# Key pages turned during the projections, a float32 forget gate, and VectorE in place of GpSimd in the 31-tap convolution

## The reference, cut to what matters

```python
# layer 0
h = rmsnorm(x, norm_mix0) @ w_in0              # gb, gc, hv, q, k, v, fl
y_a = gb * causal_dwconv(gc * hv, hist, conv_a_w)          # 3 taps
q, k = rmsnorm(q, q_norm), rmsnorm(k, k_norm)  # per head, 8 heads of 64
logf = log_sigmoid(fl + b_forget)              # fl: 8 columns of w_in0
y_b = attend(q, k, v, cumsum(logf))            # prompt: causal over 512 rows
                                               # samples: 16 pages of 128 cached keys each, and 4 new rows
x = x + concat(y_a, y_b) @ w_out0
x = x + conv_ffn(x)
# layer 1
a, g = split(rmsnorm(x, norm_mix1) @ w_pw1 + b_pw1)
u = a * sigmoid(g)
y = causal_dwconv(u, hist, conv_c_w)           # 31 taps, depthwise
x = x + silu(layernorm(y + conv_c_b)) @ w_pw2
x = x + conv_ffn(x)
```

## Time and profile before

| quantity | value |
|---|---|
| time, median of 3 runs | 1434.85 us (1431.5 to 1435.65) |
| the profiled execution's own time | 1429.25 us |
| its span | 1427.5 us |
| PE busy | 1380.1 us (97%) |
| DVE busy | 726.2 us (51%) |
| ACT busy | 441.8 us (31%) |
| POOL busy | 636.9 us (45%) |

### The profile page before, as it was taken

The page is one execution under the profiler, slowest core; times in us unless marked ns, Lnnn a source line. Parts: engine busy times, 40 slices in busy tenths (PEclk is TensorE's granted clock), DMA queues, the critical chain, the costliest instruction groups (busy, mean ns, idle before and its releaser), DMA issues. The chain is left out here.

```text
span 1427.5 us, 34112 instructions
## 1 busy us (share of the span) xinstructions
PE 1380.1 (97%) x13885; PEld 1292.8 (91%) x13885; DVE 726.2 (51%) x1236; ACT 441.8 (31%) x675; POOL 636.9 (45%) x402
## 2 busy tenths in 40 slices
PE   6998999999999999999999999988999999999998
PEld 5897777768999999999999987768999999999998
DVE  5654778774455443014443499878654430144411
ACT  4243433332333222322223432236332221222221
POOL 3322464443426554445545554432365544455441
PEclk9999999999999999999999999999999999999999
DMA  6415999988143322333314555540333223333131
GB/s 189 134 55 192 310 340 386 378 275 302 46 120 93 88 81 83 91 100 89 88 56 97 147 150 142 146 119 23 109 104 88 81 78 93 103 90 88 55 95 67
DMA packets 259649, 191.57 MB, mean 134 GB/s; under 512 B 26287, under 2 KB 219264, under 8 KB 259528
## 3 DMA queue, kind: packets, MB, share of 16 engines
q1 hardware_dynamic: 258283, 187.71, 42.9%
q0 software_dynamic: 656, 2.13, 0.5%
q10 hardware_dynamic: 605, 0.24, 0.1%
HBM read 173.03 MB, written 6.04 MB: 125 GB/s over the span
## 5 line engine op out<-in xcount | busy, mean ns | idle before, releaser
L711 POOL TENSOR_TENSOR w_l<-w_raw,w_h 128x1024 fp32r<-128x1024 f32 (+2 forms) x195 | 440.0, 2259 | 374.2 <-ACT w_h L883 356.2
L1892 PE MATMUL banks<-xa_h,w_h 128*128 128x272 f32 x1856 | 388.3, 290 | 0.4 <-issue 0.3
L1892 PE MATMUL banks<-xa_h,w_l 128*128 128x272 f32 x1856 | 384.8, 289 | 0.0
L1892 PE MATMUL banks<-xa_l,w_h 128*128 128x272 f32 x1856 | 383.4, 288 | 0.0
L1892 PEld LDWEIGHTS banks<-xa_h,w_h 128*128 128x128 f32 x1856 | 293.5, 189 | 2.4 <-issue 0.8
L1892 PEld LDWEIGHTS banks<-xa_l,w_h 128*128 128x128 f32 x1856 | 292.5, 189 | 0.0
L1892 PEld LDWEIGHTS banks<-xa_h,w_l 128*128 128x128 f32 x1856 | 290.5, 189 | 0.0
L883 ACT ACTIVATE w_h<-w_raw 128x1024 fp32r<-128x1024 f32 (+2 forms) x193 | 185.3, 961 | 195.5 <-PE banks L1892 185.8
L1892 PE MATMUL banks<-h_h,w_h 128*128 128x272 f32 x928 | 192.6, 289 | 0.5 <-DVE x L1643 0.5
L1892 PE MATMUL banks<-h_h,w_l 128*128 128x272 f32 x928 | 192.7, 289 | 0.0
L1892 PE MATMUL banks<-h_l,w_h 128*128 128x272 f32 x928 | 192.1, 288 | 0.0
(11 more groups left out here) (291 smaller groups left out, 1618.2 us busy)
## 6 DMA issues: line engine op xcount, KB each, us to landing
w_raw<-in_w_up SPq DMA_DIRECT2D x88, 512.0 KB, 3.7
k_grp<-in_cache_k SPq DMA_DIRECT2D x128, 256.0 KB, 4.6
v_pg<-in_cache_v SPq DMA_DIRECT2D x120, 256.0 KB, 5.6
w_raw<-in_w_in SPq DMA_DIRECT2D x24, 512.0 KB, 6.5
w_raw<-in_w_down SPq DMA_DIRECT2D x32, 384.0 KB, 3.3
w_raw<-in_w_pw SPq DMA_DIRECT2D x24, 512.0 KB, 4.1
w_raw<-in_w_down SPq DMA_DIRECT2D x32, 320.0 KB, 3.1
w_raw<-in_w_out SPq DMA_DIRECT2D x8, 512.0 KB, 5.4
```

What stands on the lines that cost most here:

```text
L711: g.tensor_tensor(w_l[:, slot, 0:n], w_raw[:, slot, 0:n], w_h[:, slot, 0:n].bitcast(F32), ALU.subtract).then_inc(s_lo, 1)
L1892: ins = mm(out[:, half, 0:HT], w, v[:, half * HT:(half + 1) * HT], start=first and t == 0 and n == 0, stop=last and t == phase.tiles - 1 a ...
```

## The change

1. `forget_gate` multiplies `x` itself, in full float32, by `fw_g`, the forget columns times the gain of the norm (made once by GpSimd). The 544 rows are cut into four parts of 136 (QT), and part c writes to partitions 32c to 32c+7 of one bank, so there are 32 instructions in place of 48.
2. Group 1 of the keys is loaded when slab 9 is done (two slabs earlier in `s_slab`), and VectorE turns it after slabs 10 and 11. The squares of the last head pair are summed right after those of the last but one, in another pair of banks (`last_sums`). Round 0 begins with the scores; its rows of v follow them, and the wait for the last slab's scaling stands behind the scores.
3. In the 31-tap stage SP makes the copies of `u` ahead of the weight loads; VectorE makes the low parts (two a chunk) and the tap weights (one a chunk), and `combine` is split in two, so that its first half (`taps_summed`) runs before a low part. GpSimd has only one low part and the copies for the first and the last chunk left in the loop.

The diff, cut to its core:

```diff
 LAG = 4
-ROWS_IN = {0: ((0, 1), (2,), (3, 4)), 1: ((5, 6), (7,), (8, 9))}
+ROWS_IN = {0: ((), (0, 1, 2), (3, 4)), 1: ((5, 6), (7,), (8, 9))}
...
                     elif slot == 1:
-                        sp.wait_ge(s_slab, ph["qkv"].slab1)
+                        sp.wait_ge(s_slab, ph["qkv"].slab1 - 2)
...
                 i, j = s // 4 % 4, s % 4
+                if s >= 8 and s % 2 == 0:
+                    shifted(s // 2 - 4)
...
                     n_out.extend((before_rows, n_out[0]))
-                if s >= 8 and s % 2 == 0:
-                    shifted(s // 2 - 4)
...
                 split_low(0, slot, DC)
-            pool.wait_ge(s_fw, 33)
-            g.tensor_tensor(fw_l[:, :, :], fw[:, :, :], fw_h[:, :, :].bitcast(F32), ALU.subtract).then_inc(s_fw, 1)
+            pool.wait_ge(s_fw, 32)
+            pool.wait_ge(s_gnd, 1)
+            g.tensor_tensor(fw_g[:, :, :], fw[:, :, :], params[:, 0:DC].unsqueeze(2).to_broadcast([P, DC, NH]), ALU.mult)\
+             .then_inc(s_fw, 1)
...
-            def tap_weights(c, b):
-
-                if isinstance(c, int) and c == 0:
-                    pool.wait_ge(s_cz, 2)
-                    pool.wait_ge(s_hist, 1)
-                    pool.wait_ge(s_tap, 16)
-                if not (isinstance(c, int) and c < 2):
-                    pool.wait_ge(s_cvp, c - 1)
-                g.tensor_tensor(w_sh[b][:, :, :], every32[:, :].unsqueeze(1).to_broadcast([P, 32, 32]),
-                                tap_sh[:, ds(c, 1), :, :].rearrange("p a q k -> p (a q k)").unsqueeze(2)
-                                .to_broadcast([P, 32, 32]), ALU.mult).then_inc(s_wsh, 1)
-
...
-            def turn(i, last):
-                for j in range(4):
-                    if last and j == 2:
-                        for late in (2, 3):
-                            ahead(split_low, ph["pw1"], i, late, last)
-                        tap_weights(i * 2 + 1, 1)
-                        shifted_also(DC - 1)
-                    if last and j >= 2:
-                        continue
-                    ahead(split_low, ph["pw1"], i, j, last)
-                    if isinstance(i, int) and i == 0:
-                        if j == 1:
-                            shifted_also(0)
-                        if j < 2:
-                            tap_weights(j, j)
-                    elif j % 2:
-                        tap_weights(i * 2 + j // 2, j // 2)
-            turns(pool, ph["pw1"], turn, 1)
+            split_low(ph["pw1"].slab0 // 4, 3, DC)
+            shifted_also(0)
+            shifted_also(DC - 1)
+            pool.wait_ge(s_lo, ph["pw2"].slab0 + 3)
...
                 A(sq[:, m % 2, :], x[:, m, :], ACT.Square).then_inc(s_sq, 1)
-            act.wait_ge(s_fw, 32)
-            A(fw_h[:, :, :], fw[:, :, :], ACT.Copy).then_inc(s_fw, 1)
...
                     q_blocks(0)
-                if n >= 4:
+                if 4 <= n < 11:
                     head_root(n - 4)
+                if n == 10:
+                    head_root(7)
...
                 dve.wait_ge(s_misc, 5)
-                V.tensor_tensor(fz[:, 0:HT], bank[0][0:NH, 0:HT], r_all[0:NH, 0:HT], ALU.mult).then_inc(s_dve, 1)
-                st.tick()
-                V.tensor_tensor(fz[:, HT:T], bank[1][0:NH, 0:HT], r_all[0:NH, HT:T], ALU.mult).then_inc(s_miscd, 1)
+                for c in range(4):
+                    at, rows = slice(c * QT, (c + 1) * QT), slice(32 * c, 32 * c + NH)
+                    V.tensor_tensor(fz[:, at], bank[0][rows, 0:QT], r_all[rows, at], ALU.mult)\
+                     .then_inc(s_miscd if c == 3 else s_dve, 1)
+                    if c < 3:
+                        st.tick()
...
                     forget_in()
-                if n >= 4:
+                if 4 <= n < 11:
...
                     forget_sums()
-                if n >= 4:
+                if n == 10:
+                    head_var(7)
+                if 4 <= n < 11:
                     head_norm(n - 4)
+                if n == 10:
+                    head_norm(7)
+                    key_turned(1, 0)
+                if n == 11:
+                    key_turned(1, 1)
...
                     V.memset(bank[1][:, 160:161], 1.0).then_inc(s_clr, 1)
-                if more:
+                if more and n:
                     key_turned(n + 1, 0)
-                if n == 0:
-                    key_turned(1, 1)
...
+            def low_part(s):
+
+                slot = s % 4
+                dve.wait_ge(s_hi, s + 1)
+                dve.wait_ge(s_lo, s)
+                V.tensor_tensor(w_l[:, slot, :], w_raw[:, slot, :], w_h[:, slot, :].bitcast(F32), ALU.subtract).then_inc(s_lo, 1)
+
+            def tap_weights(c):
+
+                if c == 0:
+                    dve.wait_ge(s_cz, 2)
+                    dve.wait_ge(s_tap, 16)
+                if c >= 2:
+                    dve.wait_ge(s_cvp, c - 1)
+                V.tensor_tensor(w_sh[c % 2][:, :, :], every32[:, :].unsqueeze(1).to_broadcast([P, 32, 32]),
+                                tap_sh[:, c, :, :].rearrange("p q k -> p (q k)").unsqueeze(2).to_broadcast([P, 32, 32]),
+                                ALU.mult).then_inc(s_wsh, 1)
+
...
                 dve.wait_ge(s_u, c * 2 + 2)
+                first = 2 * c + ph["pw1"].slab0 + SLOTS
+                if c:
+                    taps_summed(c - 1, 1 - b)
+                else:
+                    tap_weights(0)
+                    tap_weights(1)
+                low_part(first)
...
                     combine(c - 1, 1 - b)
+                if 1 <= c < DC - 1:
+                    tap_weights(c + 1)
...
                     st.tick()
+                if c < DC - 1:
+                    low_part(first + 1)
...
                 chunk(c // 2, c % 2)
+            taps_summed(DC - 1, 1)
...
-                pe.wait_ge(s_fw, 34)
+                pe.wait_ge(s_fw, 33)
+                pe.wait_ge(s_xnew, DC)
                 for t in range(DC):
-                    for n, (w, v) in enumerate(((fw_h, xa_h), (fw_h, xa_l), (fw_l, xa_h))):
-                        for half in range(2):
-                            ins = mm(bank[half][0:NH, 0:HT], w[:, t, :], v[:, t, half * HT:(half + 1) * HT],
-                                     start=t == 0 and n == 0, stop=t == DC - 1 and n == 2)
+                    for c in range(4):
+                        ins = mm(bank[0][32 * c:32 * c + NH, 0:QT], fw_g[:, t, :], x[:, t, c * QT:(c + 1) * QT],
+                                 start=t == 0, stop=t == DC - 1)
...
                     forget_gate()
-                if n >= 4:
-                    c = n - 4
+                for c in ((n - 4,) if 4 <= n < 10 else (6, 7) if n == 10 else ()):
                     pe.wait_ge(s_qsq, c + 1)
-                    if c:
+                    if c == 7:
+                        pe.wait_ge(s_miscd, 8)
+                    elif c:
...
                     for half in range(2):
-                        ins = mm(psum_s[:, half, 0:HT], head_ones[:, :], sq[:, c % 2, half * HT:(half + 1) * HT],
+                        ins = mm((psum_s if c < 7 else last_sums)[:, half, 0:HT], head_ones[:, :], sq[:, c % 2, half * HT:(half + 1) * HT],
...
-            pe.wait_ge(s_free, gates_s0)
+            pe.wait_ge(s_free, gates_s0 - 1)
...
                     score_group(n)
+                if n == 0:
+                    pe.wait_ge(s_free, gates_s0)
```

More of the change, by code:

```diff
@@ L21 @@
 HT = T // 2
+QT = T // 4
 NH, HD = 8, 64
@@ L220, in build @@
         fw, fw_at = place("fw", [P, DC, NH], F32)
-        fw_h, _ = place("fw_h", [P, DC, NH], F32R)
-        fw_l, _ = place("fw_l", [P, DC, NH], F32R)
+        fw_g, _ = place("fw_g", [P, DC, NH], F32)
         ext_a, _ = place("ext_a", [P, 4, NB, CA - 1 + NT], F32)
@@ L1299, in head_var @@
                     dve.wait_ge(s_qk, c - 1)
-                V.tensor_scalar(halves(tmp[:, c % 2, :]), psum_s[:, :, 0:HT], 1.0 / HD, EPS, ALU.mult, ALU.add)\
+                V.tensor_scalar(halves(tmp[:, c % 2, :]), (psum_s if c < 7 else last_sums)[:, :, 0:HT], 1.0 / HD, EPS, ALU.mult, ALU.add)\
                  .then_inc(s_hv, 1)
@@ L1751, in _, with taps_summed @@
                 V.memset(u_sh[n][:, :, 0:3], 0.0).then_inc(s_cz, 1)
-            def combine(c, b):
+            def taps_summed(c, b):
                 after()
@@ L1770, in combine @@
                      .then_inc(s_sqp, 2 if c == 2 else 1)
+            def combine(c, b):
+                n0 = DVE_SHIFTS[0]
                 dve.wait_ge(s_cvp, c + 1)
```

1 line of the change is left out of this document (added).

## The result

Before: 1434.82 us, median of 4 executions (1431.5 to 1435.65). Changed: 1419.95 us, median of 4 (1418.56 to 1423.08). The ratio is 0.9898 (95% interval 0.9878 to 0.9917), so the change gives 14.9 us; 14.2 had been forecast. The profiled execution of the changed kernel took 1420.63 us, that of the kernel before 1429.25: the two traces differ by 8.6 us only.

What follows compares the result with a forecast made beforehand. TensorE, 97% busy, was taken as the bound, its time being work plus waits. Gains of 4.1 + 6.1 + 4.0 = 14.2 us from a 1434.85 us median gave 1420.6 us; 8-in-10 range 1415 to 1431.

Steps and rivals of the forecast that it cites:

- the value pages' row: Forget gate: sixteen value-page products of the same form take 1.06 us, scaled to 2.25 us for the new gate.
- 2.38 times: Forget gate: the Trainium skill's speedup for small products in three groups; by it the gate takes 3.7 us, saving 2.7.
- with nothing beside them: Forget gate before: its 48 instructions were read as taking 6.4 us of TensorE alone.
- The wait named as next: After the last key scores: TensorE, after two row tiles, waits some 0.6 us for the bank ScalarE copies.
- GpSimd's chain: After slab 11: high part, low part and key bias take 4.5 us; TensorE needs the result some 6.5 us after.
- Rival 2: Rounds after the earlier keys: DMA queue sets the pace, losing 0 to 6.1 us; all lost gives 1426.7; chance 0.15.
- X: 31-tap stage: time of one 1024-element VectorE instruction, taken as 1.2 us; VectorE binds from 1.47.
- the loads, some 11 us later: 31-tap stage: weight loads placed behind the copies of `u` still have a period and more until their slab.
- Rival 4: 31-tap stage keeps its waits since copies, not `u`, are late: 4.0 us less gain, 1424.6 us; chance 0.13.
- The three terms: Forecast gains: forget gate 4.1 us, earlier keys 6.1 us, 31-tap stage 4.0 us.
- its own signs: Checks: gate 2 to 2.5 us, `u` copy waits near 0, chunks at 17.3 us; wrong if the clock falls elsewhere.
- the formula: 31-tap stage: VectorE's chunk takes 12.9 + 3X us, against TensorE's 17.3 us.

Runs made afterwards that it cites:

- the part alone: The kernel before with only the changed 31-tap stage: 1428.31 us, ratio 0.9966 (0.9952 to 0.9979).
- the gate alone: The kernel before with only the float32 forget gate in four column groups: 1433.31 us, ratio 0.9988 (0.9967 to 1.0009).
- the first two parts: The kernel before with the float32 forget gate and the earlier keys, the 31-tap stage left as before: 1426.34 us, ratio 0.9939 (0.9917 to 0.996).

## Why the prediction was right

**The gate.** Forecast 2.25 us and a gain of 4.1, measured 1.98 and 3.9. Scaling the value pages' row was right, and 2.38 times (3.7 us) was not what happened: four groups gave 3.75. The 6.4 us of before were not "with nothing beside them": the first instruction began 0.45 us into the one ahead of it, where it now begins after 0.95. That takes 0.5 us off the gain, and 0.27 comes back since 2.25 was too high. That the gain passes on is not shown. Alone it was worth 1.7 us (−1.3 to 4.7), and undoing the groups cost 2.2 instead of 5.4.

**The keys.** Forecast 6.1 and 11.5 us from slab 11's end to round 1, measured 6.5 and about 11. The wait named as next (TensorE for ScalarE's copy, 0.6) is there with 0.58; GpSimd's chain cost nothing. Rival 2 said that DMA would give the gain back. Its mechanism acted elsewhere: no key was late, but instructions were, 3.2 us in this trace. Since two kernels with the old rounds had the same wait, it is no price of this part. The part measured 7.0 us by its ratio, and 5.0 without its three executions at 1417 us.

**The 31-tap stage.** Forecast 4.0, measured 4.2 in the loop, 4.9 by the time of the part alone and 4.8 by its trace against the gate alone. X was 1.22 us, for the tap weights too, and the chunks follow at 17.4 us. The step that failed is the one on the loads: "the loads, some 11 us later". That is true of chunks in the loop. In the last one the low part stands right behind `u`, the load follows it 2.6 us after the copies' start, and there is no slab between `u` and the taps to hide it. Holding the load back gives 4.0 to 4.6 us from the first taps to the second product. Rival 4 (the copies are late) was so right for one chunk in eight, for a reason that I had not given. And the 4 us are the price of one rhythm of the old stage, not of its work.

**The sum.** 14.2 forecast, 14.9 and 13.9 measured. The three terms hold within a microsecond or so, but that the sum does has luck in it. The late copies of the last chunk and the late instructions in round 2 were not foreseen. They don't show in the time, since the kernel before mostly loses as much: its stage, where the gate alone and the first two parts have it, takes 5 us more than in its profiled execution, and its rounds, in two of three traces, 3.6 and 4.15 us more. The terms were read from that one good execution, and starting the sum from the median and not from it covered the difference. By its own signs the prediction was partly wrong: the waits for the copies are 2.8 us and not near 0, and the clock fell elsewhere (0.88 from 130 to 140 us).

## What to carry to other kernels

An operand's small copies and a bulk load should not be in flight together where the next step waits for the copies; look at the last turn of a loop by itself, since work that spaced them in the middle is missing there. Before moving work from GpSimd to VectorE, add up VectorE's turn with the new passes in it and compare it with the pace of the bound engine: the formula was right to 0.1 us a chunk. One trace of a kernel can be a lucky one: before a loss is put down to a change, look for the same stretch in other traces that share its code. A wait without an operand ("issue") can be checked against the packets of the instruction queue.

## What the runs showed that I had not expected

- Float32 instructions with 8 weight columns in four column groups run 3.75 times as fast as in one (1.98 against 7.43 us for the same product).
- TensorE can stand 0.7 to 2.2 us for its own instructions while the DMA engines are busy 0.87 of their time and more; it goes on 1.25 to 1.49 us after the packet with them ends, and in most of these traces its clock falls behind the wait. With a share of 0.65 the packet was in time, and once with 1.04 as well.
- The same stage's code takes 104.2 or 108.3 to 108.5 us from first to seventh taps by which of GpSimd and VectorE starts first, and 129.5, 133.8 or 138.9 us to the second product; three of twelve executions of one kernel were over 8 us under all the others, and the trace of one of them had the undisturbed rhythm.
